# Raw transposes for the second mixer's norm, one queue for x, and later loads of output weights in a two-layer decoder trunk

## What is computed

```
def rms_norm(x, g, eps=1e-6):
    return x * rsqrt(mean(x * x, -1) + eps) * g
def reference(x, ...):
    h = x                                              # (1, 256, 1024)
    for layer in range(2):
        u = rms_norm(h, norm_mix[layer])
        if layer == 0:
            cols = u @ hyb_w_in
            mix = concat([rwkv7_mix(cols[:1696]), nsa_mix(cols[1696:])]) @ hyb_w_out
        else:
            mix = mamba2_mix(u, ssm_w_in, ...)         # z, xbc, dt = split(u @ w_in)
        h = h + mix                                    # xbc = silu(conv(xbc)); dt = softplus(dt + bias)
        h = h + hier_moe(rms_norm(h, norm_ffn[layer]), ...)
    return rms_norm(h, norm_final)
```

## Time and profile before

| what | value |
|---|---|
| median of 3 runs | 1321.83 us (1320.2 to 1322.5) |
| the profiled execution | 1320.47 us |
| its span, first to last instruction | 1318.7 us |
| PE busy, instructions | 1220.1 us (93%), 8776 |
| PEld busy, instructions | 673.4 us (51%), 8776 |
| DVE / ACT / POOL busy | 400.1 / 271.0 / 40.7 us |
| read from HBM | 461.06 MB, 350 GB/s over the span |
| instruction packets of the queue q8 | 73 |
| chain that ended last | PE 64%, DMA 26%, DVE 4%, issue 2%, ACT 2% |
| mean granted TensorE clock | 0.971 |

### The profile page before, as it was taken

One profiled execution on the slowest core, in us unless ns is written; L12 is line 12 of the kernel. 1 busy time (PEld: TensorE's weight loads), 2 busy tenths in 40 slices (PEclk: granted clock), 3 DMA queues, 4 the chain that ended last, 5 costly groups with the idle time before them and its releaser, 6 DMA issues.

```text
span 1318.7 us, 20861 instructions
## 1 busy us (share of the span) xinstructions
PE 1220.1 (93%) x8776; PEld 673.4 (51%) x8776; DVE 400.1 (30%) x1016; ACT 271.0 (21%) x558; POOL 40.7 (3%) x34
## 2 busy tenths in 40 slices
PE   9999999999999888798999999999999997787987
PEld 4777755444443333443588887454444443333433
DVE  1287856121112111111247655152121112101111
ACT  1343523111010000000233656031101110000102
POOL 1003200000000000000000111000000000000000
PEclk9999999999999989798999999999999999887989
DMA  7633289999999999999944474979999999999996
GB/s 270 209 104 161 85 344 392 428 427 425 428 427 426 427 427 428 424 426 425 359 163 176 160 287 166 408 274 426 425 428 429 426 425 429 427 427 424 426 428 266
DMA packets 55898, 463.62 MB, mean 352 GB/s; under 512 B 8624, under 2 KB 9936, under 8 KB 26608
## 3 DMA queue, kind: packets, MB, share of 16 engines
q1 hardware_dynamic: 55792, 462.16, 85.3%
HBM read 461.06 MB, written 1.08 MB: 350 GB/s over the span
## 4 chain that ended last, share of the span: by engine, by line
PE 64%; DMA 26%; DVE 4%; issue 2%; ACT 2%; SPq 1%; another core or an unknown queue 1%; DVEq 0%; ACTq 0%
DMA raw<-in_moe_w_up 18%; PE bank L2262 9%; DMA raw<-in_moe_w_gate 7%; PE bank L2243 6%; PE bank L2923 5%; PE sums L2309 5%; PE bank L2199 5%; PE sums L2923 4%; PE bank L3055 4%; PE bank L2300 4%; PE bank L2287 3%; PE bank L1264 3%; PE bank L1296 2%; PE bank L2273 2%; SPq L332 1%
## 5 line engine op out<-in xcount | busy, mean ns | idle before, releaser
L2262 PE MATMUL bank<-raw,xg 128*32 128x512 f32 x1664 | 232.6, 647 | 50.9 <-DMA raw<-in_moe_w_up 44.9
L2172 DVE TENSOR_TENSOR aT<-bank,sg 128x128 f32<-128x128 f32 (+1 forms) x64 | 20.2, 316 | 550.6 <-ACT sg L2067 550.6
L2262 PEld LDWEIGHTS bank<-raw,xg 128*32 128x32 f32 x1664 | 59.0, 118 | 199.3 <-issue 117.6
L2199 PE MATMUL bank<-sel,ux 128*128 128x64 f32 (+1 forms) x896 | 117.7, 288 | 13.3 <-DVE sel L2089 12.4
L2199 PEld LDWEIGHTS bank<-sel,ux 128*128 128x128 f32 x896 | 110.9, 202 | 37.0 <-issue 21.6
L2309 PE MATMUL sums<-ys,selT 64*128 64x512 f32 x512 | 127.2, 615 | 1.6 <-DVE ys L2185 1.6
L2064 ACT COPY gus<-bank 128x512 f32<-128x512 f32 x64 | 37.5, 585 | 440.0 <-PE bank L2262 334.9
L2300 PE MATMUL bank<-raw,aT 128*32 128x512 f32 x832 | 100.1, 598 | 9.4 <-DVE aT L2172 9.4
L2309 PEld LDWEIGHTS sums<-ys,selT 64*128 64x128 f32 x512 | 44.2, 186 | 84.1 <-issue 80.0
L2243 PE MATMUL bank<-raw,xg 128*64 128x512 f32 x384 | 84.7, 594 | 0.0
L2923 PE MATMUL bank<-uT,wr 128*128 128x256 f32 x352 | 78.2, 381 | 0.0
(11 more groups left out here) (438 smaller groups left out, 1236.6 us busy)
## 6 DMA issues: line engine op xcount, KB each, us to landing
raw<-in_moe_w_gate SPq DMA_DIRECT2D x54, 2048.0 KB, 40.7
raw<-in_moe_w_up SPq DMA_DIRECT2D x54, 2048.0 KB, 45.2
raw<-in_moe_w_down SPq DMA_DIRECT2D x54, 2048.0 KB, 45.1
raw<-in_moe_w_gate SPq DMA_DIRECT2D x20, 1024.0 KB, 11.4
raw<-in_moe_w_up SPq DMA_DIRECT2D x20, 1024.0 KB, 10.7
raw<-in_moe_w_down SPq DMA_DIRECT2D x20, 1024.0 KB, 10.1
wr<-in_ssm_w_in SPq DMA_DIRECT2D x10, 2048.0 KB, 8.5
odd<-in_hyb_w_in SPq DMA_DIRECT2D x2, 2048.0 KB, 10.3
```

The source lines that it names most:

```text
L2199: i = T.matmul(bank[SIDE_BANK][:, k * n:(k + 1) * n].rearrange("p (x s) -> p x s", x=2), ux[:, t, 4 * half + k, :], src[:, t, :, :], start ...
L2262: i = T.matmul(bank[GU_BANK][CAP_S * c:CAP_S * c + CAP_S, :], xg_f[:, x, 4 * half + k, :], raw[:, slot, k * FH:(k + 1) * FH], start=(half ...
```

## The change

It has three parts, and small matters of storage that go with them.

1. The start: ScalarE issues the load of the identity, now together with the gain `mix0`, which moves from `feat` to the constant table. SP starts with x and issues `feat` behind the weights. VectorE no longer waits for `feat` before the first evictions, but before the constants.
2. The four loads `w2` wait for `products` of level 2, 3, 4 and 5.
3. The second norm: the gain row `mix1` and its load are gone; the gain is in `feat`. VectorE and ScalarE copy sums to h, one side each. TensorE transposes h (four groups, order `TURNS2`), VectorE evicts three of them times gain to `uTr` and ScalarE the fourth in four pieces. The dt product and the first projection take the raw `uTr`. Between the two halves of that projection the inverse root is spread over the partitions (`spread_root`, row `rb2`). VectorE and POOL then scale `uTr` to `uT2` (five and three tiles) for all later projections; VectorE scales the first projection's result and the dt result as it reads them. The two filler matmuls are gone.

```diff
     @block.sync
     def _(sp):
-        load(sp, "ident", cst[:, 0:P], a["tables"][:, 0:P])
         load(sp, "x", h[:, 0, :], a["x"][0, 0:P, :])
         load(sp, "x1", h[:, 1, :], a["x"][0, P:SEQ, :])
-        load(sp, "feat", feat[:, :], a["feat"])
         for k, name in ((0, "w0a"), (2, "w0b"), (4, "w0c"), (6, "w0")):
...
             load(sp, name, wr[1][:, k:k + 4, :], w_hyb[1][:, k:k + 4, :])
+        load(sp, "feat", feat[:, :], a["feat"])
...
-        for k, free in enumerate((None, 1, 2, 3)):
-            if free is not None:
-                sp.wait_ge(*at("prod", free, 1))
+        for k, level in enumerate((2, 3, 4, 5)):
+            sp.wait_ge(*at("prod", level, 1))
             load(sp, "w2", ...)
...
         dve.wait_ge(s_ld["ident"], 16)
-        dve.wait_ge(s_ld["feat"], 16)
...
-                                   rep(FT("mix0")[:, 4 * q:4 * q + 4], P, 2), ALU.mult), "read", "turn", "mix0", t, q)
+                                   rep(C("mix0")[:, 4 * q:4 * q + 4], P, 2), ALU.mult), "read", "turn", "mix0", t, q)
...
+        dve.wait_ge(s_ld["feat"], 16)
         dve.wait_ge(s_ld["small"], 32)
...
     @block.scalar
     def _(act):
         A = nc.scalar
+        load(act, "ident", cst[:, 0:FIRST], a["tables"][:, 0:FIRST])
         act.wait_ge(*at("consts"))
...
     def mixer_ahead(sp, b0):
...
-        gain_ahead(sp, b0, "mix1")
         for n in range(3):
             load_group(sp, n)
...
     @block.gpsimd
     def _(pool):
         G = nc.gpsimd
+        for t, q in TURNS2:
+            pool.wait_ge(*at("read", "turn", "mix1", t, q))
+        pool.wait_ge(*at("read", "rb2"))
+        G.tensor_tensor(uT2[:, 5:8, :], uTr[:, 5:8, :], rep(rb2, 3), ALU.mult).then_inc(pool_done, PO.one(("uTs2", 1)))
         router_weighted(pool, 1)
...
-        dve.wait_ge(s_ld["gain"], 16 * (NORMS.index("mix1") + 1))
-        sums_weighted(dve, "mix1", u2, 0, 0)
-        sums_part(dve, "mix1", 0, ss2, ss2[:, 2 * HALVES:])
-        sums_weighted(dve, "mix1", u2, 0, 1)
-        sums_weighted(dve, "mix1", u2, 1, 0)
-        sums_part(dve, "mix1", 1, ss2, ss2[:, 2 * HALVES:])
-        inverse(dve, "mix1", 0, std2, rstd2)
-        diagonal(dve, "mix1", 0, rstd2)
-        sums_weighted(dve, "mix1", u2, 1, 1)
-        inverse(dve, "mix1", 1, std2, rstd2)
-        diagonal(dve, "mix1", 1, rstd2)
+        for t in range(HALVES):
+            dve.wait_ge(*at("h", "mix1", t))
+            go(V.tensor_copy(h[:, t, side(0)], sums[:, t, side(0)]), "read", "sums", t, 0)
+        for t, q in TURNS2[0:1] + TURNS2[2:4]:
+            dve.wait_ge(*at("turn", "mix1", t, q))
+            go(V.tensor_tensor(uTr[:, 4 * q:4 * q + 4, t * P:(t + 1) * P],
+                               bank_of("turn", "mix1", t, q)[:, :].rearrange("p (k t) -> p k t", k=4),
+                               rep(FT("mix1")[:, 4 * q:4 * q + 4], P, 2), ALU.mult), "read", "turn", "mix1", t, q)
         V.memset(xr[:, :, :, 0:3], 0.0).then_inc(dve_done, DV.one(("xr0",)))
         for t in range(HALVES):
-            go(V.tensor_copy(h[:, t, :], sums[:, t, :]), "read", "sums", t)
+            inverse(dve, "mix1", t, std2, rstd2)
+            diagonal(dve, "mix1", t, rstd2)
+        dve.wait_ge(*at("read", "turn", "mix1", *TURNS2[1]))
+        dve.wait_ge(*at("read", "rb2"))
+        go(V.tensor_tensor(uT2[:, 0:5, :], uTr[:, 0:5, :], rep(rb2, 5), ALU.mult), "uTs2", 0)
+        dve.wait_ge(*at("xbc", *XJ[0]))
+        go(V.tensor_tensor(xr[:, 0, :, 3:SEQ + 3], bank_of("xbc", *XJ[0])[:, :].rearrange("p (c t) -> p c t", c=2),
+                           rep(rb2, 2), ALU.mult), "read", "xbc", *XJ[0])
...
-        sums_act(act, "mix1", junk2[:, 0:BANK], ss2, ss2[:, 2 * HALVES:], std2)
-        turn_act(act, "mix1", uT2, KD)
+        for t in range(HALVES):
+            act.wait_ge(*at("h", "mix1", t))
+            A.copy(h[:, t, side(1)], sums[:, t, side(1)]).then_inc(act_done, AC.one(("read", "sums", t, 1)))
+        t, q = TURNS2[1]
+        act.wait_ge(*at("turn", "mix1", t, q))
+        for k in range(4):
+            A.activation(uTr[:, 4 * q + k, t * P:(t + 1) * P], bank_of("turn", "mix1", t, q)[:, k * P:(k + 1) * P],
+                         ACT.Identity, scale=FT("mix1")[:, 4 * q + k:4 * q + k + 1]).then_inc(act_done, AC.one())
+        new[("read", "turn", "mix1", t, q)] = ("act", AC.n)
+        for t in range(HALVES):
+            act.wait_ge(*at("read", "sums", t, 0))
+            act.wait_ge(act_done, AC.n)
+            square_act(act, h[:, t, :], junk2[:, :], ss2, t)
+            act.wait_ge(act_done, AC.n)
+            A.activation(std2[:, t:t + 1], ss2[:, t:t + 1], ACT.Sqrt, scale=1.0 / D, bias=eps_n[:, 0:1]).then_inc(
+                act_done, AC.one(("std", "mix1", t)))
+        act.wait_ge(*at("rb2"))
+        A.copy(rb2, bank_of("rb2")[:, 0:SEQ]).then_inc(act_done, AC.one(("read", "rb2")))
...
+        def spread_root():
+
+            b = take(pe, "rb2")
+            for t in range(HALVES):
+                pe.wait_ge(*at("u", "mix1", t))
+                i = T.matmul(b[:, t * P:(t + 1) * P], C("ones"), diag[:, t, :], start=True, stop=True)
+            i.then_inc(pe_done, PE.one(("rb2",)))
...
-        for j in range(2):
-            T.matmul(bank[SIDE_BANK][:, :], ident, cst[:, 0:BANK], start=True, stop=True)
-        turn_pe(pe, "mix1", u2, KD, pool=FREE)
+        for t, q in TURNS2:
+            b = take(pe, "turn", "mix1", t, q, pool=FREE)
+            pe.wait_ge(*at("read", "sums", t, q))
+            for k in range(4):
+                i = T.transpose(b[:, k * P:(k + 1) * P], h[:, t, (4 * q + k) * P:(4 * q + k + 1) * P], ident)
+            i.then_inc(pe_done, PE.one(("turn", "mix1", t, q)))
         pe.wait_ge(s_ld["small"], ring0["small"] + 48)
-        pe.wait_ge(*at("read", "turn", "mix1", 1, 1))
         b = take(pe, "dtq")
-        for k in range(KD):
-            q = MH * (k % 4)
-            i = T.matmul(b[q:q + MH, 0:SEQ], wdt[:, k, :], uT2[:, k, :], start=(k < 4), stop=(k >= KD - 4))
+        for half in (1, 0):
+            for t in range(HALVES):
+                pe.wait_ge(*at("read", "turn", "mix1", t, half))
+            for k in range(4 * half, 4 * half + 4):
+                q = MH * (k % 4)
+                i = T.matmul(b[q:q + MH, 0:SEQ], wdt[:, k, :], uTr[:, k, :], start=(half == 1), stop=(half == 0))
         i.then_inc(pe_done, PE.one(("dtq",)))
-        project(0, 0)
+        project(0, 0, src=uTr, between=spread_root)
...
+        pe.wait_ge(*at("uTs2", 0))
+        pe.wait_ge(*at("uTs2", 1))
         project(0, 1)
```

71 lines of the change are left out of this document (32 added, 39 removed).

## The result

In the first comparison the changed kernel takes 1312.37 us (median of 4 runs, 1312.06 to 1313.46) against 1322.16 for the kernel before (4 runs, 1320.20 to 1322.69). The ratio is 0.9925, 95% interval 0.991 to 0.994: faster by 0.6 to 0.9%. Times 1321.83, the median shown ahead of the prediction, it gives 1311.9 us. Over all comparisons, 40 executions of the kernel before have the median 1321.8 and 10 of the changed one 1313.1: 8.7 us, 95% interval 7.3 to 9.7 by resampling.

The account below looks back on a forecast made before the run. Expert layers were bound by DMA at 427 GB/s, their stream released by TensorE and VectorE. Savings of 1.1 + 2.15 + 4.2 = 7.45 us took the profiled 1320.47 to 1313.0; with 1.36 added, median 1314.4, range 1312.3 to 1317.8.

Parts of the forecast that it names:

- Part 1: Kernel start: first projection at 7.6 to 7.65 instead of 8.73, 1.1 us earlier; bounds 0.4 and 1.4.
- Part 2: First mixer, output-weight loads: later issue removes TensorE's 2.15 us stall, an instruction block behind 1 MB; bounds 0 and 2.3.
- Single bursts cause no stall: First mixer: 512 KB bursts at levels 2 and 3 cause no stall, so spread loads would cause none.
- The last of the four loads: First mixer, output weights: issue estimated at 153, wanted by TensorE at 163.46, so 6 us of slack.
- Part 3: Second mixer: projection 4.65 us earlier, less 0.45 for the root's row, net 4.2; bounds 2.8 and 5.2.
- w0: Second mixer's weights: without gain's load they land at 648.5 to 649.2, just about meeting the projection at 649.1.
- The diagonals: Second mixer, before the root's row: ready at 651.5, TensorE comes at 652.6, so 1.1 us of slack.
- the scaled copy: Second mixer, for later projections: POOL's 768 columns take 1.75 us, done at 655.4, needed at 657.0, slack 1.6.
- The clock rivals: Second mixer at half clock: once in 645 to 649, 1317.3 us, chance 0.04; over the projections, 1328.6, chance 0.02.
- The rival's line that 10 us at half rate: Second mixer's low-clock rival, chance 0.02: kernel ends slower once TensorE works over 10 us at half rate.
- The rival that the stream swallows parts 1 and 2: Expert layers: the weight stream absorbs the earlier gains, leaving only 4.2 us, total 1317.6; chance 0.07.
- the last term of the sum: Whole kernel: the median lies 1.36 us above the profiled execution, so 1313.0 becomes 1314.4.

Follow-up runs that it names:

- w2_burst: The changed kernel with all four loads of output weights (2 MB) after level 3 instead of 2, 3, 4 and 5; 1316.65 us in one execution.
- pool_first: The changed kernel with VectorE's part of the scaled copy held until GpSimd's part is done; 1312.32 us in one execution.
- upper_first: The changed kernel with the first projection taking tiles 4 to 7 first and one more scaled-copy tile on VectorE; 1314.51 us in one execution.
- after_again: The changed kernel unchanged, timed again against the kernel before in more rounds; median 1314.03 us, ratio 0.9932 (0.9914 to 0.995).

## Why the prediction came out as it did

- **Part 1, forecast 1.1, measured 1.16.** The price is right, and the bounds hold. The reason was half right: I had the first piece of weights at 7.6 as the next thing. In the changed kernel the projection follows TensorE's turns at 7.57 and no load. In three others with the same start (w2_burst, pool_first, upper_first) it starts at 7.17 to 7.23 and its row names the weights, after 0.28 us of waiting. The two are level, and either can come last.
- **Part 2, forecast 2.15 with bounds 0 and 2.3, measured 2.4.** The cause, inferred from one stand and one missing packet, is now shown by two experiments and by the packets' times. The mis-sized term is the stand: the "issue" of the row is not the whole loss. The group around it took 3.56 us against 1.12 after, 2.44 more, and my upper bound lay below that. "Single bursts cause no stall" was too strong as well: one 512 KB load still cost 0.87 us where a block was due. The Trainium skill, page "Runtime: NRT & Kernel Launch", section "Instruction fetch mechanics", calls the crossing of a block mostly hidden. That held in the quiet stretches here, and not behind a burst of loads (0.87, 2.15 and 2.56 us).
- **The last of the four loads**, estimated to be issued at 153, was issued at 149.20. It never bound.
- **Part 3, forecast 4.65 less 0.45, 4.2 in all.** Measured: the first projection 10.26 less 5.49, so 4.77 sooner; the root's row 0.45; at the third projection 4.21 in all. Against the other kernels with the old mixer it is 3.8. w0, forecast 5.0 to 5.7 us after the last scatter's start (648.5 to 649.2), was in after 5.15; gain's own share of the queue, put at 1.35 by its bytes, measured 1.34 in one pair of executions and 1.4 on average. The diagonals were there at 648.13 and TensorE came at 649.33: 1.2 us of slack where I had 1.1.
- **A step of part 3 that failed without a price** is the scaled copy: "So 1.75 for its 768 ... done at 655.4, and needed at 657.0: 1.6 us of slack". I priced GpSimd from a row of 23.77 to 28.42 us in which VectorE executes nothing, and beside VectorE it took 3.10. The slack was 0.09 us. It didn't show in the time only because TensorE was no earlier.
- **The clock rivals fell.** From 641 to 654 us the granted clock is 1.00, with 16 transposes in place of 32 passes of plain matmuls and the two fillers. This is 2.4 GHz all along, so the rule of the Trainium skill (page "TensorE: Matmul & The Clock Gate", section "Part 4: PE-mode transpose") that transposes are no activity took nothing here; but the stretch is short and stands between dense ones, so it doesn't refute the rule. The rival's line that 10 us at half rate would use up the gain was a wrong sum: 7.45 us of work would have to be done at half rate, which takes 14.9.
- **The rival that the stream swallows parts 1 and 2** fell too: the first expert layer took 417.62 and 417.73 us, so it moved as a whole.
- **The whole.** By the stretches outside the expert layers the change is worth 483.96 less 476.49, that is 7.47 us, against 7.45 forecast. That agreement is partly luck: part 2 had 0.3 more, and the second "issue" gave 0.29 back. In after_again, where that one lasts 0.19 us, the same sum is 8.1. The runs say 8.7 (7.3 to 9.7).
- **The step that missed the time** is the last term of the sum: "The median of the runs, 1321.83, is 1.36 above that execution, so it becomes 1314.4." The profiled execution was forecast at 1313.0 and took 1313.46, so everything up to this term is right to 0.5 us. But the median of the changed kernel's four executions, 1312.37, lies 1.09 below its profiled one, and in after_again 0.09 below. I had taken the distance of one execution from its median for something that belongs to the kernel and moves with it. It was a short execution of the kernel before: 40 of them have the median 1321.8, 1.3 above it. This term is 2.45 us off; the 0.46 of the profiled execution goes the other way, and 2.0 us are left between 1314.4 and 1312.37. The range had no term for it either. Its low end, 2.1 us under the forecast, left out that a median of four executions of each kernel moves by 1 to 2 us against another, which the trace of one execution can't show. How far the first comparison fell outside is chance: its 1311.9 lies 0.4 below the range, and with the 8.7 us of all comparisons it would be 1313.1, inside.
- **What stays open.** The two expert layers together took between 834.4 and 838.1 us in the fourteen profiled executions, of either kind of kernel (834.7 in the kernel before, 835.2 in the changed one, 836.4 in after_again). Nothing there makes them longer in the kernel before: the four kernels with the old second mixer have 835.7 on average, the ten with the new one 835.7 too. So the gap between 7.5 and 8.7 has no place in the traces, and 7.5 lies within the runs' interval; whether it is chance isn't settled, since timed executions leave no trace.

## What to carry to other kernels

Where TensorE stands in the middle of a dense group with no semaphore open, look for a burst of loads issued just before and for the instruction packet that is missing. Spread the burst, and count the slowed group around the stand as well as the stand itself. Before work is split between VectorE and GpSimd, ask what a single VectorE takes for all of it: here 2.29 us against 3.17 for both. Before a median is forecast from one profiled execution, ask how far that execution lies from its own kind; here 1.3 us of the distance were its own. And cut the spans at common marks before believing a sum of medians: stretches that the change doesn't touch agreed to 0.1 us where they were bound by TensorE, and varied by 1 to 3 us where they were bound by DMA.

## What the runs showed of the hardware

- **GpSimd gave way to VectorE almost entirely.** With two operands in SBUF each, GpSimd's 768 columns took 1.81 us alone and 3.10 beside 1.49 of VectorE; 512 took 2.82 beside 1.76. The excess is 1.29 us there, a little less than VectorE's own time, and VectorE, which started 0.06 us earlier, lost nothing. The Trainium skill, page "SBUF — State Buffer", section "Who interferes with whom", says that the pair of ports that the two share is an exclusive lock, and that a VectorE instruction with two SBUF inputs contends with a GpSimd instruction that reads SBUF; that the second of the two fully blocks it says of VectorE's two-port modes. The traces agree, nearly with full blocking here too: 1.42 us until VectorE is done and 1.81 alone would be an estimate of 3.2, where I had 1.75 and 3.10 was measured.
- **Instruction blocks wait behind data.** In a stretch where TensorE takes a packet about every 4 us, loads of 0.5 MB made it stand for 0.87 us, of 1 MB for 1.69 to 2.15 and of 2 MB for 2.56. In all of these it went on 2.2 to 2.5 us after the packet of its next block; where the packet came 2.7 us or more ahead of use there was no stand.
- **The clock can fall behind such a stand.** After 2.56 us it was 0.50 (1.2 GHz) for some 3 us; after 2.15 us it stayed at 1.00.
- **A load of 512 KB ahead of another costs its bytes** (1.34 us in one pair of executions, 1.4 on average over fourteen kernels), even behind the small rows of the dt weights. Landing times without it scatter by 1.2 us from one execution to the next.
